# Bidirectional attention and gated linear attention on one core: products with q moved to GpSimd, token-major outputs, a new rope order

## What is computed

```python
q = apply_axial_rope(rms_norm(q, q_norm), ang_r, ang_c)      # 8 heads of 64
k = apply_axial_rope(rms_norm(k, k_norm), ang_r, ang_c)      # 2 heads of 64
s = einsum("bqkgd,bskd->bkgqs", qblk, k) * HEAD_DIM ** -0.5
o = einsum("bkgqs,bskd->bqkgd", softmax(s), v)

# gated linear attention (GLA), 4 heads, dk 64, dv 128, chunks of 64, forward and backward
b = cumsum(g)                                                 # log decay
A = einsum("bhtd,bhsd,bhtsd->bhts", q, k, exp(b_t - b_s) where s <= t)
o = A @ v + (q * exp(b)) @ S;  S = exp(b_last) * S + (k * exp(b_last - b)).T @ v
o = rms_norm(o_f + o_b, gla_norm) * silu(r)
```

## Time and profile before

| | us |
|---|---|
| median of 3 runs | 2629.57 (2619.59 to 2638.2) |
| the profiled execution: time | 2638.64 |
| the profiled execution: span | 2636.8 |
| TensorE busy | 2313.7 (88% of the span) |
| VectorE busy | 925.2 (35%) |
| ScalarE busy | 666.6 (25%) |
| GpSimd busy | 324.3 (12%) |
| mean granted TensorE clock | 0.916 of full speed |

### The profile page before, as it was taken

One profiled execution on the slowest core, in us unless ns is written; L12 is line 12 of the kernel. 1 busy time (PEld: TensorE's weight loads), 2 busy tenths in 40 slices (PEclk: granted clock), 3 DMA queues, 4 the chain that ended last, 5 costly groups with the idle time before them and its releaser, 6 DMA issues. The chain is left out here.

```text
span 2636.8 us, 37017 instructions
## 1 busy us (share of the span) xinstructions
PE 2313.7 (88%) x15383; PEld 2121.1 (80%) x15383; DVE 925.2 (35%) x1838; ACT 666.6 (25%) x1252; POOL 324.3 (12%) x276
## 2 busy tenths in 40 slices
PE   5996889996778889975999859999999999999598
PEld 5995778885567777945888749999999999999476
DVE  4204660002578755245337641111111111112354
ACT  3211221112545455224323210010000110012254
POOL 0111121212033411000000000000100100001100
PEclk9998999998878888657999869999999999999799
DMA  3213332213000010017322167687776876774321
GB/s 129 97 61 110 123 126 80 82 56 142 13 13 13 16 62 13 13 28 230 109 98 96 64 239 267 240 285 247 231 272 238 282 257 224 265 262 150 88 80 60
DMA packets 177296, 359.99 MB, mean 137 GB/s; under 512 B 11121, under 2 KB 52721, under 8 KB 174833
## 3 DMA queue, kind: packets, MB, share of 16 engines
q1 hardware_dynamic: 156224, 280.75, 30.3%
q0 software_dynamic: 20912, 76.95, 9.4%
HBM read 298.03 MB, written 59.64 MB: 136 GB/s over the span
## 5 line engine op out<-in xcount | busy, mean ns | idle before, releaser
L1899 PE MATMUL ps<-e_x,e_raw 128*128 128x160 f32 x4096 | 562.9, 300 | 1.0 <-DVE e_x L2031 1.0
L1899 PEld LDWEIGHTS ps<-e_x,e_raw 128*128 128x128 f32 x4096 | 558.8, 190 | 1.4 <-DVE e_x L2031 1.4
L1899 PE MATMUL ps<-e_h,e_raw 128*128 128x160 f32 x2048 | 292.7, 299 | 0.0
L1899 PEld LDWEIGHTS ps<-e_h,e_raw 128*128 128x128 f32 x2048 | 281.6, 190 | 0.0
L1203 DVE TENSOR_REDUCE a_stat<-ps 128x1 f32<-128x1024 f32 (+1 forms) x80 | 85.0, 1063 | 386.5 <-PE ps L907 386.4
L1986 ACT ACTIVATE aff_hidden<-ps 128x160 f32<-128x160 f32 x128 | 38.9, 304 | 522.2 <-PE ps L1899 522.2
L926 PEld LDWEIGHTS ps<-v_tok,a_ptr 128*128 128x128 f32 x1088 | 139.5, 206 | 30.4 <-ACT a_ptr L1041 19.6
L926 PE MATMUL ps<-v_tok,a_ptr 128*128 128x64 f32 x1088 | 148.5, 292 | 12.6 <-ACT a_at L1049 6.4
L593 PE MATMUL ps<-act_hi,w_hi 128*128 128x512 f32 (+1 forms) x600 | 152.2, 362 | 7.5 <-PEq L251 7.5
L916 PE MATMUL ps<-ident,a_p 128*128 128x128 f32 x544 | 99.0, 335 | 63.5 <-ACT a_p L1034 63.4
L593 PE MATMUL ps<-act_lo,w_hi 128*128 128x512 f32 (+1 forms) x600 | 151.2, 360 | 0.0
(11 more groups left out here) (306 smaller groups left out, 3804.5 us busy)
## 6 DMA issues: line engine op xcount, KB each, us to landing
e_raw<-in_w_gate_e SPq DMA_DIRECT2D x32, 2048.0 KB, 8.1
e_raw<-in_w_up_e SPq DMA_DIRECT2D x32, 2048.0 KB, 12.3
e_raw<-in_w_down_e SPq DMA_DIRECT2D x32, 2048.0 KB, 9.1
w_raw<-in_w_blk SPq DMA_DIRECT2D x18, 1024.0 KB, 4.9
fm_scratch<-fm_out POOLq DMA_DIRECT2D x25, 640.0 KB, 3.2
early<-fm_scratch SPq DMA_DIRECT2D x80, 128.0 KB, 3.9
tm_scratch<-tm_out POOLq DMA_DIRECT2D x50, 128.0 KB, 2.0
n_x<-in_x SPq DMA_DIRECT2D x10, 512.0 KB, 3.6
```

The lines of the kernel that those rows point to most:

```text
L1899: last = pe.matmul(ps[:, bank, 0:CAP], raw[slot][:, k, part * P:(part + 1) * P], src[:, k, :], start=(k == 0), stop=(k == KT - 1))
```

## The change

Five things change together.

- In `walk`, the transposes run two tiles behind instead of one, and `turn_k` moves from behind a tile's products to their middle (after four of the eight k slices). Token tiles are rotated in the order 2 to 9, 0, 1 (`ROPED`), SP loads two tiles ahead, and the ten broadcasts of the gains become one.
- The last two rotated tiles, 0 and 1, stay in the SBUF buffer `q2`, which now lives through both stages; they are neither stored nor loaded.
- The factor `HD ** -0.5` is multiplied into q when it is evicted, so the row maximum is used as the bias directly and L1205 goes.
- In the levels GpSimd does the product with q (one instruction of 2560 columns) in front of that with k; VectorE's two go.
- `out_mm` swaps its operands, so outputs come token-major: 128 moving columns in place of 64 for the state products. ScalarE squares per head with a sum (40 of 128 columns); `ss_mm`, the ones and the diagonal go. VectorE multiplies a pair's outputs by the reciprocal root (`normalise_heads`), TensorE transposes them (`turn_final`, four transposes a pair), and `final` is one instruction. The finals start at hook 66 in place of 68.5.

```diff
         def walk(split, turn_q, rope, fm, turn_k):
             for n, (j, half) in enumerate(tiles):
-                if 1 <= n <= NT:
-                    turn_q(n - 1)
+                if 2 <= n <= NT + 1:
+                    turn_q(n - 2)
                 if half == 0 and j + 1 < BLOCKS:
                     split(nth(TM_BLOCKS + j + 1))
                 if n < NT:
                     rope(n, n % 2, n // 2)
+                if 2 <= n <= NT + 1:
+                    turn_k(n - 2)
                 fm(n, nth(TM_BLOCKS + j), half)
-                if 1 <= n <= NT:
-                    turn_k(n - 1)
...
                 for k in range(KT):
+                    if k == KT // 2 and 2 <= n <= NT + 1:
+                        turn_k(n - 2)
...
-                    dve.tensor_tensor(at, turned(part)[rows], at.bitcast(F32), ALU.subtract).then_inc(lo_done, 1)
+                    dve.scalar_tensor_tensor(at, turned(part)[rows], SCALE, at.bitcast(F32), ALU.mult, ALU.subtract).then_inc(lo_done, 1)
...
-                if h == 0:
-                    pe.wait_ge(q_in[t % 2], 16 * (t // 2 + 1))
+                if h == 0 and t >= 2:
+                    pe.wait_ge(q_in[t % 2], 16 * (t // 2))
...
-                        if l < NL:
-                            dve.wait_ge(S["lvl_exp"], l + 1)
-                            dve.wait_ge(S["q_scaled"], 1)
-                            dve.tensor_tensor(ql[l % 2][:, h, :], ql[l % 2][:, h, :], q[:, h, :], ALU.mult).then_inc(S["lvl_q"], 1)
...
                 pool.wait_ge(S["lvl_exp"], l + 1)
+                pool.wait_ge(S["q_scaled"], 1)
+                pool.tensor_tensor(flat(ql[l % 2]), flat(ql[l % 2]), flat(q), ALU.mult).then_inc(S["lvl_q"], 1)
                 pool.tensor_tensor(flat(kl_[l % 2]), flat(kl_[l % 2]), flat(k), ALU.mult).then_inc(S["lvl_k"], 1)
...
-                        pe.matmul(slot(B0 + h % 2, pair, h), v[:, a, h * DV:(h + 1) * DV], att[:, a, h, :], start=True, stop=False,
+                        pe.matmul(slot(B0 + h % 2, pair, h), att[:, a, h, :], v[:, a, h * DV:(h + 1) * DV], start=True, stop=False,
...
-                            last = pe.matmul(slot(B0 + h % 2, pair, h)[:, j * CHUNK:(j + 1) * CHUNK], state[d][rows, c, h // 2, :],
-                                             (ql[1], kl_[1])[d][rows, h // 2, t], start=False, stop=(i == len(terms) - 1),
+                            last = pe.matmul(slot(B0 + h % 2, pair, h)[j * CHUNK:(j + 1) * CHUNK, :], (ql[1], kl_[1])[d][rows, h // 2, t],
+                                             state[d][rows, c, h // 2, :], start=False, stop=(d, j) == max(x for x in terms if x[1] == j),
...
+                def turn_final(a):
+                    pe.wait_ge(S["norm_done"], a + 1)
+                    pe.wait_ge(S["final"], a)
+                    for h in range(GLA_H):
+                        last = pe.transpose(ps[:, B2, h * P:(h + 1) * P], out[:, a, h, :], core.ident[:, :])
+                    last.then_inc(S["ft_tr"], 1)
...
-                    act.activation(sq[:, 2 * n:2 * n + 2, :, :], out[:, 2 * n:2 * n + 2, :, :], ACT.Square).then_inc(S["sq_done"], 1)
+                    for i, (a, h) in enumerate(TWO):
+                        if i == 4:
+                            yield two_out(n) + 1.5
+                        col = (2 * n + a) * GLA_H + h
+                        last = act.activation(squares[:, 2 * n + a, h, :], out[:, 2 * n + a, h, :], ACT.Square, accum_out=stat[:, 0, col:col + 1])
```

More of the change, by code:

```diff
@@ L37 @@
 HEADS, KV_HEADS, HD = 8, 2, 64
+SCALE = HD ** -0.5
 QKV_W = (HEADS + 2 * KV_HEADS) * HD
@@ L63 @@
 LEVELS = (32, 16, 8, 4, 2, 1)
+ROPED = [*range(2, NT), 0, 1]
 class Chain:
@@ L476, in _, with rope @@
         def _(sp):
-            def rope(t, b, use):
+            def rope(n):
+                b, use, t = n % 2, n // 2, ROPED[n]
                 sp.wait_ge(out_done[b], use)
@@ L483, in rope @@
                 sp.dma_start(tab[:, b, :, :], io["rope"][t]).then_inc(x_in[b], 16)
-            for h in range(HEADS):
-                sp.dma_start(gain[:, h, :], io["q_norm"].partition_broadcast(P)).then_inc(s_const, 16)
-            for h in range(KV_HEADS):
-                sp.dma_start(gain[:, HEADS + h, :], io["k_norm"].partition_broadcast(P)).then_inc(s_const, 16)
-            walk(lambda blk: ring.load(sp, blk), skip, rope, skip, skip)
+            rope(0)
+            sp.dma_start(gain[:, :, :].rearrange("p h d -> p (h d)"), io["qk_norm"].partition_broadcast(P)).then_inc(s_const, 16)
+            rope(1)
+            walk(lambda blk: ring.load(sp, blk), skip, lambda n, *_: rope(n + 2) if n + 2 < NT else None, skip, skip)
             sp.wait_ge(v_in, 16 * NT)
@@ L527, in turn_q @@
                     act.wait_ge(tr_done, 3 * t + part + 1)
-                    act.activation(q2[:, t % 2, 4 * part:4 * part + 4, :], turned(part), ACT.Copy).then_inc(hi_done, 1)
+                    act.activation(q2[:, t % 2, 4 * part:4 * part + 4, :], turned(part), ACT.Copy, scale=SCALE).then_inc(hi_done, 1)
             def turn_k(t):
                 act.wait_ge(tr_done, 3 * t + 3)
-                act.activation(kh[:, :, tokens(t)], turned(2), ACT.Copy).then_inc(hi_done, 1)
+                act.activation(kh[:, :, tokens(ROPED[t])], turned(2), ACT.Copy).then_inc(hi_done, 1)
             walk(lambda blk: ring.high(act, blk), turn_q, rope, fm, turn_k)
@@ L626, in upto, with stage_attention_beside_gla @@
             self.next = next(self.program, self.END)
-def stage_attention_beside_gla(core, kh, kl, v_tok, split_up, spare):
+def stage_attention_beside_gla(core, kh, kl, v_tok, q2, split_up, spare):
     nc, io = core.nc, core.io
@@ L655, in stage_attention_beside_gla @@
         one = lambda prefix, names: {n: core.sem(prefix + n) for n in names.split()}
-        A = one("a_", "s_done max_done bias_done exp_done t_done t_read pv_done rc_done o_done ot_done ot_read")
+        A = one("a_", "s_done max_done exp_done t_done t_read pv_done rc_done o_done ot_done ot_read")
         q_in = core.kept_sems("a_q_in", 2)
@@ L675, in stage_attention_beside_gla @@
         mask = sb("g_mask", [P, len(LEVELS) + 1, P], I32)
-        ones = sb("g_ones", [P, P])
         gain = sb("g_gain", [P, 1])
@@ L690, in stage_attention_beside_gla @@
         kt = [diff[d].rearrange("p h t -> p (h t)").rearrange("p (a h c) -> p a h c", a=PAIRS, h=HP) for d in range(2)]
-        ps_ss = ps[:, 7, 0:PAIRS * GLA_H]
         by_pair = lambda x: whole(x).rearrange("p (a h c) -> p a h c", a=PAIRS, h=GLA_H)
-        out, sq = by_pair(both), by_pair(turns[0])
-        diag = [whole(bcum)[:, b * 512:(b + 1) * 512] for b in range(2)]
+        out, gated = by_pair(both), by_pair(turns[0])
+        squares = by_pair(bcum)
         flat = lambda a: a.rearrange("p h t -> p (h t)")
@@ L752, in store_final @@
                 for h in range(GLA_H):
-                    sp.dma_start(core.up_in[KT // 2 + h, :, a * P:e * P].rearrange("p (a c) -> p a c", c=P), out[:, a:e, h, :]
+                    sp.dma_start(core.up_in[KT // 2 + h, :, a * P:e * P].rearrange("p (a c) -> p a c", c=P), gated[:, a:e, h, :]
                                  ).then_inc(S["stored"], 16)
@@ L855, in out_mm @@
                     a = 2 * n + pair
-                    chunks_of = lambda d: [j for j in range(2) if 2 * a + j not in FIRSTS[d]]
-                    terms = [(d, j) for j in range(2) for d in range(2) if j in chunks_of(d)]
+                    terms = [(d, j) for d in range(2) for j in range(2) if 2 * a + j not in FIRSTS[d]]
                     for h in (2 * hp, 2 * hp + 1):
-                        pe.matmul(slot(B0 + h % 2, pair, h), v[:, a, h * DV:(h + 1) * DV], att[:, a, h, :], start=True, stop=False,
+                        pe.matmul(slot(B0 + h % 2, pair, h), att[:, a, h, :], v[:, a, h * DV:(h + 1) * DV], start=True, stop=False,
                                   skip_group_check=True)
@@ L870, in out_mm @@
                         last.then_inc(S["out_mm"], 1)
[L872 to L889 removed]
+                def turn_final(a):
[4 more added lines that the diff above has]
+                    last.then_inc(S["ft_tr"], 1)
                 items = [(out_at(n, m), out_mm, (n, m)) for n in range(TWOS) for m in range(4)]
[L892 to L893 removed]
+                items += [(final_at(a), turn_final, (a,)) for a in range(PAIRS)]
                 for hook, emit, args in sorted(items, key=lambda item: item[0]):
@@ L1071, in gla @@
                 yield 0
-                dve.memset(ones[:, :], 1.0).then_inc(S["ones_done"], 1)
                 for u in range(2 * HP):
@@ L2304, in host_inputs @@
     out["g_mix"] = w["g_mix"][0]
-    for name in ("q_norm", "k_norm", "w_router", "w_gate_e", "w_up_e", "w_down_e", "w_out", "w_ple_gate", "w_ple_proj",
+    out["qk_norm"] = np.concatenate([w["q_norm"][0]] * HEADS + [w["k_norm"][0]] * KV_HEADS)
+    for name in ("w_router", "w_gate_e", "w_up_e", "w_down_e", "w_out", "w_ple_gate", "w_ple_proj",
                  "g_moe", "g_ple"):
```

94 lines of the change are left out of this document (34 added, 60 removed).

## The result

The changed kernel takes 2535.7 us (median; the kernel before beside it on the same chip 2624.6): a ratio of 0.9661, 95% interval 0.9615 to 0.9708. The forecast was 2548, with a range of 2515 to 2580.

A forecast was written before the change was run, and what follows sets the result against it. TensorE, busy for most of the span, was taken as the bound, so edits pay only where it waits or loses instructions. Terms -30.5 - 4.8 - 4 - 0 - 42 = -81.3 gave 2548 us against the median 2629.6; range 2515 to 2580.

The forecast's parts named there:

- Levels: Attention beside GLA, six levels: moving q products to GpSimd only shifts the stall one unit on; 0 us (+6 to -25).
- Token-major outputs: GLA outputs and prompt units: TensorE loses 49.2 us of sums, spreading and waits, gains 7.3 of transposes; -42 (-26 to -52).
- up to 10 us: GLA output stage: possible clock gain without the one-column sums of squares, left in the range and not in the sum.
- no wait takes the place of the 16.1: Prompt units: VectorE's loop (some 2.4 us) stays under TensorE's own work (2.9 us), so the 16.1 us of diagonal waits vanish.
- Rope order: Projection stage: TensorE's waits of 17.5 and 18.0 us go, 5 us come back; -30.5 us (-24 to -35.5).
- five split steps: Projection steps 2, 4, 6, 8 and 9, with a weight split: VectorE runs over by 1.0 us each, 5 us back.
- q tiles: Start of attention: first scores no longer wait for q to come back from memory; -4.8 us (-2 to -6).
- The scale: Between row maximum and exponential: one-column multiplication goes, some 0.2 us in 22 units where TensorE waits; -4 (-2 to -7).
- Rival 1: Levels: VectorE's subtractions miss GpSimd's run, so the moved products pay 25 us; 2523 us in all; chance 0.13.
- rival 2: GLA outputs: 128-column matmuls don't overlap or the clock stays at 1.2 GHz; some +30, 2578 us; chance 0.12.
- rival 3: Projection stage: VectorE bounds the rope loop in every step, eight waits of about 2 us; about 2560 us; chance 0.06.
- rival 4: GLA units: TensorE falls to its lower clock, some 4 us more per unit; slower, about 2660 us; chance 0.03.

## Why the prediction came out as it did

**Levels (0; measured +1.4).** Right, and by its own steps: the length of both subtractions, the row maxima 11 us apart, TensorE's 5.6 us. The +1.4 is itself a sum: +3.6 from the products (209.5 - 205.9 in the kernel before with that edit alone) and about -2 from the scale, whose step costs 3 us or more there. What the forecast did not see is what the edit is good for: the stall that moved sits at an instruction that can be joined and put behind the normalisation, and then some 36 us come (207.3 to 171.1, with the last subtraction too). With the product back on VectorE, at the one place tried, 22 us go again (177.6 to 199.7, without the last one).

**Token-major outputs (-42; measured -57.9).** The mechanism was right; the term of the state products was mis-sized, and so was the clock's gain. "I expect about nothing, and take 0" stood against the row that had just this tile (L842, 0.050 us each), and the row was set aside for its better clock. The old price, 17.8/144 = 0.124, counts time twice: 25.4 us for 288 is 0.088 each. With L842's row that gives 288 x (0.050 - 0.088) = -11; the products fell from 25.4 to 13.2 us, -12.2, of which some 7 at equal clock.

The clock's gain, left in the range as "up to 10 us", was nearer to 20: over units 57 to 79 the mean granted clock rose from 0.68 to 0.83. Some 5 us of it are in the state products, 3.7 in the products with `att` (16.5 to 12.8 us, 0.66 for four in both kernels at a clock of 1.00), and 10.7 in attention's own scores, transposes and products with v, whose shapes no edit changes (77.4 to 66.7 us). That the clock rises with this edit is shown by the kernel that has it alone (0.85 over these units, against 0.69 in that with the q products alone); why it does isn't shown. Two smaller misses go the other way: the 40 transposes took 9.5 us, not 7.3, and "no wait takes the place of the 16.1" is wrong by 6.8 us, in front of L877. Sum: -49.2 + 9.5 + 6.8 - 12.2 - 3.7 - 10.7 = -59.5, with 1.6 us of small waits and overlaps against it. Squares at 0.300 + 0.193 = 0.49 us (0.47 forecast) and the units 70 to 75 at 3.5 to 4.1 us came as forecast.

**Rope order (-30.5; measured -26.4).** The sum was near, its account was not. The 1.0 us taken for each of five split steps was too dear: with the weights early, four waits make 2.6 us. The 9.9 us were in no term: the forecast replayed VectorE's and ScalarE's queues, but not SyncE's, which holds the weight block behind loads that now run one tile further ahead. Measured is -35.5 for the two old waits, +12.1 for the new ones and -3.0 since TensorE was busy for less time (370.0 to 367.0 us, granted clock 0.97 to 0.98). With the weights early it is -35.5 + 2.6 - 4.7 (365.3 us, clock 1.00) = -37.6. No run has the order, the middle place of `turn_k` and the one broadcast singly.

**q tiles (-4.8; measured -5.1)** as forecast. **The scale (-4)** can't be seen in the long stretches of the two profiles, which show +0.5 over units 0 to 57; the single units and the run that undoes it bear its sign out.

Against this sum of -81.3, the trace has -94.8 (the medians -88.9). Of the 13.5 us between, 15.9 are the outputs; 5.9 lie behind unit 79, which no edit touches and which scatters by some 6 us between executions; the rope and the scale's stretches take 8.6 back. That the total came within 13 us of the forecast is partly luck: its misses have opposite signs.

Rival 1 (levels pay) and rival 2 (outputs cost) are refuted by the single edits, rival 3 (the rope bound in every step) by the trace: beside the 9.9 us there are three waits, 2.2 us together. Of rival 4 one piece is in the trace: behind the stall in a level TensorE runs at a granted 0.58 (the unit of 8.2 us, 846.92 to 855.10). But it did so in the kernel before, at 0.50 (871.40 to 877.80), and the whole level is only 0.4 us longer.

## What to carry to other kernels

When an instruction moves from VectorE to GpSimd and both work out of SBUF, replay the queues and look for the next VectorE instruction with two SBUF operands: the stall can move there, as it did here. Count such meetings, join them, and put each behind what another engine waits for. When a load is issued further ahead, go down the queue that issues it and ask what stands behind its wait. And price a changed matmul shape by the row that has its tile; a better clock in that row is a reason for a range, not for zero.
